# Two transformer blocks on one core: the last two output slabs by token halves, and the norm by pairs of chunks

## The chip, the cores and the metric

The kernel runs on one core of one Trainium2 chip. The metric is the device time of one execution in microseconds (us), lower is better. Each kernel is run several times and the median is given.

## What is computed

The reference runs two models one behind the other on 512 tokens with 1024 features, all in fp32. The first has two layers: a gated delta-net mixer and then a latent-attention (MLA) mixer, each followed by a gated feed-forward network (FFN). The second has one layer: retention and sliding-window attention merged by gates, and again an FFN. Around each of them stands the same pattern:

```python
h = rmsnorm(x, g) * (1.0 + scale) + shift
y = mixer(h)
x = x + gate * y
h = rmsnorm(x, g2) * (1.0 + scale2) + shift2
x = x + gate2 * swiglu(h, w_gate, w_up, w_down)
```

`rmsnorm` divides each token's vector by the root of the mean of its squares over the 1024 features. The second model has no shift and takes, in front of it, two norms in a row (the first model's final one and its own first one).

## The kernel before

**Layout.** x lies transposed in SBUF: 8 chunks (KC) of 128 features on the partitions, 512 tokens in the free dimension. A product of fp32 quality is made of three matmuls: every operand is split into a rounded high part and the low rest (`hi`, `lo` for weights, `hH`, `hL` for the normed activation, `aH`, `aL` for the hidden one), and lo*H, hi*L and hi*H are added up in PSUM. The weights come as slabs of 128x2048 (256 output features). SP loads a slab into `raw`, ScalarE rounds it to `hi` (`split_hi`, L362), VectorE subtracts to `lo` (`split_lo`, L366). There are two buffers of each (`raw0/1`, `hi0/1`, `lo0/1`) and two PSUM tiles D0 and D1 for slabs; D2 holds the sums of squares. `ones` times the squares on TensorE gives the sum over features on all partitions (`ones_half`, L583).

**Order.** There is no scheduler: each engine's program is written out by hand, and counting semaphores tie them together. `lo_ready` counts slabs whose low part is ready, `slab_done` slabs whose products are done, `out_half` the first halves of a junction's last slab, `x_added` and `bank_free` chunks added to x, `fsq_ready` squares, `fold_ready` folds, `fss_ready` sums, `xg_ready` normed chunks, `hh_ready` and `h_ready` high and low parts of the activation.

**A junction.** Six times a block ends with four output slabs (N_OUT) and the residual add, and a norm follows; five times the first slab of the next block follows that. In order of the program they are called here by what comes in front of or behind them: G_GOUT (n = 1, norm of the first FFN behind it), G_MIN (n = 2, the end of the first FFN and the norm of the MLA mixer), G_MOUT (n = 3), G_RET (n = 4, two norms in a row, two sums of squares at once), G_ROUT (n = 6), and the kernel's end (n = 7). The functions are `final_pe`, `final_act`, `final_dve` for the four slabs, `close_act`, `close_dve` for the norm (`last_act`, `last_dve` at the end), `product_halves` (L321) for the next block's first slab.

The first three slabs are multiplied with all 512 tokens per matmul (L301 to L303 in `product`), the last one by halves of 256 tokens (L611 to L613), so that the first half's norm can start while the second half is multiplied. VectorE adds a slab's two chunks to x (L557, by halves L721); ScalarE squares them (L619) into `af` or `sg`; VectorE folds the squares of two slabs into one (L644) and, before the last slab, the two chunks of the fold into one (L649). `ones_half` of a half adds one matmul of the fold and two of the last slab's squares. Then ScalarE takes Ln (L667) and Exp (L669) to get the reciprocal root for 256 tokens.

The norm handles 16 pieces (2 halves of tokens by 8 chunks, 128x256 each). For each of them VectorE multiplies x with gain and root into `nq` (L735), ScalarE adds the shift and rounds to `hH` (L706) and, where the next block's product by seven quarters wants the whole value (n = 1, 3, 6), writes it once more unrounded to `tR` (L708, L705), and VectorE adds the shift to `nq` again and subtracts `hH` to get `hL` (L742). `product_halves` waits for each piece's `h_ready`. `nq` has four places.

**Weights around a junction.** With slab 4 the first of the next block and slab 5 its second, `final_act` and `final_dve` split slabs 2, 3 and 4 while slabs 0, 1 and 2 are added; `close_act` rounds slab 5 at piece 6 of 16, `close_dve` takes its low part when all pieces are done. At the kernel's end slab 4 is a dummy of zeros, loaded and split like any other.

## Time and profile before

| | us |
|---|---|
| median of 3 runs | 2347.21 |
| lowest, highest | 2346.96, 2348.32 |
| the profiled execution | 2349.4 |
| its span, first to last instruction | 2347.6 |
| TensorE busy | 2266.1 (97%) |
| VectorE busy | 1401.0 (60%) |
| ScalarE busy | 1042.5 (44%) |
| GpSimd busy | 366.7 (16%) |

In the profile PE is TensorE, DVE VectorE, ACT ScalarE, POOL GpSimd. A matmul's duration in the records contains its way through the array, so matmuls overlap there: what one costs in a row of many is the distance from start to start. The same holds, to a smaller degree, for VectorE and ScalarE instructions that follow each other without a wait.

### The profile page before, as it was taken

To read this page: it belongs to the slowest core of one execution; us is meant where nothing else is said; L and a number is where in the kernel's file an instruction comes from. 1 tells how busy PE (TensorE), PEld (TensorE's weight loads), DVE (VectorE), ACT (ScalarE), POOL (GpSimd) and SP (SyncE) were. 2 spreads that over 40 slices of the span, in tenths; PEclk is the share of its full clock that TensorE was granted. 3 is DMA by queue.
4 is the path that set the end of the run, shared out by engine and by line. 5 is a ranking of instruction groups with operands and counts; after the bars stand their busy time and mean duration, and the time that the engine had idled before them with its cause. 6 is when DMAs were issued, how large, how long until landed. Compare 5 with 4: busy or idle time off the path is not lost.

```text
span 2347.6 us, 34925 instructions
## 1 busy us (share of the span) xinstructions
PE 2266.1 (97%) x14369; PEld 1920.9 (82%) x14369; DVE 1401.0 (60%) x1800; ACT 1042.5 (44%) x1568; POOL 366.7 (16%) x164
## 2 busy tenths in 40 slices
PE   6999999999999999999999999999999999999998
PEld 4777888878889986668998998888777788898897
DVE  4856755543347765547883676645367345984484
ACT  4546553443215444435552455334255325553352
POOL 0346447347790000000000000000000000000000
PEclk9999999999999999999999999999999999999999
DMA  7433232334452324311333233212211222233232
GB/s 294 143 116 135 100 135 91 118 115 181 181 210 90 109 73 163 130 67 54 109 108 117 83 124 110 85 62 72 90 55 56 89 90 72 91 108 126 90 108 90
DMA packets 40762, 260.56 MB, mean 111 GB/s; under 512 B 4432, under 2 KB 6832, under 8 KB 10416
## 3 DMA queue, kind: packets, MB, share of 16 engines
q1 hardware_dynamic: 40624, 258.59, 30.3%
q8 instruction: 103, 1.69, 0.3%
q14 instruction: 35, 0.29, 0.0%
HBM read 256.42 MB, written 2.15 MB: 110 GB/s over the span
## 4 chain that ended last, share of the span: by engine, by line
PE 79%; DVE 8%; ACT 5%; issue 2%; POOL 2%; DMA 0%; DVEq 0%; ACTq 0%
PE D L301 10%; PE D L303 10%; PE D L302 10%; PE D L1638 7%; PE D L1640 7%; PE D L1639 7%; PE D L1403 2%; PE D L2866 2%; PE D L1405 2%; PE D L1404 2%; DVE lo L366 1%; PE D L2868 1%; PE D L2867 1%; PE D L1422 1%; ACT hi L362 1%
## 5 line engine op out<-in xcount | busy, mean ns | idle before, releaser
L366 DVE TENSOR_TENSOR lo<-raw,hi 128x2048 fp32r<-128x2048 f32 (+3 forms) x131 | 288.9, 2205 | 200.4 <-ACT hi L362 200.2
L362 ACT ACTIVATE hi<-raw 128x2048 fp32r<-128x2048 f32 (+3 forms) x131 | 230.1, 1756 | 328.6 <-PE D L303 240.0
L301 PE MATMUL D<-hH,lo 128*128 128x512 f32 x560 | 227.3, 406 | 5.6 <-DVE lo L366 5.6
L303 PE MATMUL D<-hH,hi 128*128 128x512 f32 x560 | 220.9, 394 | 0.0
L302 PE MATMUL D<-hL,hi 128*128 128x512 f32 x560 | 220.9, 394 | 0.0
L1638 PE MATMUL D<-tH,lo 128*128 128x256 f32 x768 | 216.3, 282 | 0.5 <-issue 0.5
L1640 PE MATMUL D<-tH,hi 128*128 128x256 f32 x768 | 216.3, 282 | 0.0
L1639 PE MATMUL D<-tL,hi 128*128 128x256 f32 x768 | 216.2, 282 | 0.0
L375 POOL TENSOR_TENSOR adar<-adar 128x1024 f32<-128x1024 f32 (+2 forms) x120 | 213.2, 1777 | 9.4
L373 POOL TENSOR_TENSOR adar<-adar,small 128x2048 f32<-128x2048 f32 x40 | 154.0, 3850 | 326.5 <-DVE zi L1289 189.0
L1638 PE MATMUL D<-hH,lo 128*128 128x256 f32 x576 | 162.6, 282 | 2.3 <-ACT D L1721 2.3
L1640 PE MATMUL D<-hH,hi 128*128 128x256 f32 x576 | 162.1, 282 | 0.0
L1639 PE MATMUL D<-hL,hi 128*128 128x256 f32 x576 | 162.1, 281 | 0.0
L301 PE MATMUL D<-aH,lo 128*128 128x512 f32 x390 | 154.5, 396 | 0.0
L302 PE MATMUL D<-aL,hi 128*128 128x512 f32 x390 | 154.0, 395 | 0.0
L303 PE MATMUL D<-aH,hi 128*128 128x512 f32 x390 | 153.9, 395 | 0.0
L1638 PEld LDWEIGHTS D<-tH,lo 128*128 128x128 f32 x768 | 144.6, 188 | 1.1 <-issue 0.9
L1639 PEld LDWEIGHTS D<-tL,hi 128*128 128x128 f32 x768 | 144.6, 188 | 0.2
L1640 PEld LDWEIGHTS D<-tH,hi 128*128 128x128 f32 x768 | 144.6, 188 | 0.0
L301 PEld LDWEIGHTS D<-hH,lo 128*128 128x128 f32 x560 | 105.5, 188 | 32.8 <-DVE lo L366 7.2
L302 PEld LDWEIGHTS D<-hL,hi 128*128 128x128 f32 x560 | 105.5, 188 | 25.6 <-issue 2.4
L303 PEld LDWEIGHTS D<-hH,hi 128*128 128x128 f32 x560 | 105.4, 188 | 24.7
(537 smaller groups left out, 5481.7 us busy)
## 6 DMA issues: line engine op xcount, KB each, us to landing
raw<-in_slabs SPq DMA_DIRECT2D x185, 1024.0 KB, 4.8
adar<-in_ada SPq DMA_DIRECT2D x42, 1024.0 KB, 4.8
fw<-in_ada SPq DMA_DIRECT2D x6, 1024.0 KB, 24.0
x<-in_xin SPq DMA_DIRECT2D x2, 1024.0 KB, 8.9
dt<-bcast SPq DMA_DIRECT2D x8, 256.0 KB, 3.2
dtb<-bcast SPq DMA_DIRECT2D x8, 256.0 KB, 3.5
qd<-bcast SPq DMA_DIRECT2D x8, 256.0 KB, 3.7
out<-x SPq DMA_DIRECT2D x8, 256.0 KB, 2.2
```

The lines of the kernel that those rows point to most:

```text
L301: T_.matmul(o, lo[s.slot][:, w], H[:, k, :], start=(k == 0), stop=False)
L302: T_.matmul(o, hi[s.slot][:, w], L[:, k, :], start=False, stop=False)
L303: last = T_.matmul(o, hi[s.slot][:, w], H[:, k, :], start=False, stop=(k == kc - 1))
L362: S_.activation(hi[s.slot][:, 0:n], raw[s.slot][:, 0:n], ACT.Copy).then_inc(hi_ready, 1)
L366: V_.tensor_tensor(lo[s.slot][:, 0:n], raw[s.slot][:, 0:n], hi[s.slot][:, 0:n], ALU.subtract).then_inc(lo_ready, 1)
L373: chain.link(nc.gpsimd.tensor_tensor(r3, r3, cact.unsqueeze(2).to_broadcast([P, KC, 2 * P]), ALU.mult))
L375: last = nc.gpsimd.tensor_tensor(r3[:, 0:n], r3[:, 0:n], r3[:, n:2 * n], ALU.add)
L1403: T_.matmul(o, lo[s % 2][:, c], hH[:, k, :], start=(k == 0), stop=False)
L1404: T_.matmul(o, hi[s % 2][:, c], hL[:, k, :], start=False, stop=False)
L1638: T_.matmul(to, w(lo, k), H(k), start=(fresh and k == 0), stop=False, skip_group_check=True)
L1639: T_.matmul(to, w(hi, k), L(k), start=False, stop=False, skip_group_check=True)
L1640: last = T_.matmul(to, w(hi, k), H(k), start=False, stop=(k == 3), skip_group_check=True)
```

## The change

**Halves.** TensorE now takes the last two slabs by halves of the tokens, both first halves first: first half of slab 2, first half of slab 3, second half of slab 2, second half of slab 3. `out_half` counts two per junction.

**Squares.** The squares of slabs 0 and 1 are folded as before. The squares of slab 2 are folded in by halves (`half_fold_dve`); for the first half the two chunks of the fold are then folded once more into one of 256 columns, for the second half they are not. `ones_half` of the first half has 1 + 2 matmuls and stands after 36 of 48 matmuls of slab 2's second half; that of the second half has 2 + 2 and stands, as before, behind three chunks of the next block's first slab.

**Norm.** It goes by 8 pairs of chunks instead of 16 pieces. For n = 1, 2, 3 ScalarE writes a pair with the shift added to `tR` (two instructions) and rounds it to `hH` as one copy of 128x2x256; for n = 6, without a shift, VectorE writes `tR` itself and ScalarE only copies; for n = 4 VectorE multiplies with the root alone (one instruction of two chunks) and ScalarE applies the gain as it rounds. `hL` is one subtraction of two chunks (n = 4: two instructions). `h_ready` counts pairs.

**Weights.** Slab 4 is split in the norm instead of before it: ScalarE behind pair 0, VectorE behind pair 0's low part and the add of slab 2's second half. ScalarE rounds slab 5 behind all pairs. The dummy slab at the end is neither loaded nor split.

```diff
+            for h in range(2):
+                for j in range(N_OUT - 2, N_OUT):
+                    s = Slab(base + j)
+                    if h == 0:
+                        pe.wait_ge(lo_ready, s.plus(1))
+                        pe.wait_ge(bank_free[s.slot], s.prior())
+                    for m in range(2):
+                        o = D[s.slot][:, h, m * HT:(m + 1) * HT]
+                        for k in range(kc):
+                            if (h, j, m * kc + k) == (1, N_OUT - 2, 12):
+                                ones_half(pe, f, 0)
...
         def ones_half(pe, f, h):
-            pe.wait_ge(fold_ready, 3 * f + 3)
+            pe.wait_ge(fold_ready, 4 * f + h + 3)
             for q, (a, b) in enumerate(sums_of(f)):
                 o = D[2][:, h, q * HT:(q + 1) * HT]
-                T_.matmul(o, ones, a[:, 0, TH[h]], start=True, stop=False)
+                for m in range(h + 1):
+                    T_.matmul(o, ones, a[:, m, TH[h]], start=(m == 0), stop=False)
                 for m in range(2):
-                    pe.wait_ge(fsq_ready, 10 * f + 6 + 2 * h + m + 1)
+                    pe.wait_ge(fsq_ready, 12 * f + 4 * h + m + 7)
                     last = T_.matmul(o, ones, b[:, m, TH[h]], start=False, stop=(m == 1))
...
+            def pair(p):
+                act.wait_ge(xg_ready, XG[n] + p + 1)
+                if n == 4:
+                    for m in range(2):
+                        c = 2 * (p % 4) + m
+                        last = S_.activation(of_pair(hH, p)[:, m, :], norm_pair(p)[:, m, :], ACT.Identity, bias=shift(c),
+                                             scale=gain(c))
+                else:
+                    if n != 6:
+                        for m in range(2):
+                            last = S_.activation(whole_pair(p)[:, m, :], norm_pair(p)[:, m, :], ACT.Identity,
+                                                 bias=shift(2 * (p % 4) + m))
+                        last.then_inc(whole_ready, 1)
+                        act.wait_ge(whole_ready, WHOLE[n] + p + 1)
+                    last = S_.activation(of_pair(hH, p), whole_pair(p), ACT.Copy)
+                last.then_inc(hh_ready, 1)
             S_.preload_act_table_set("natural_log_exp_and_others")
-            half_squares_act(act, base, f, 0)
+            half_squares_act(act, base, f, 0, N_OUT - 1)
             half_rstd_act(act, f, n, 0)
...
+            pair(0)
+            split_hi(act, Slab(base + N_OUT))
+            half_squares_act(act, base, f, 1, N_OUT - 2)
+            pair(1)
+            pair(2)
+            half_squares_act(act, base, f, 1, N_OUT - 1)
+            pair(3)
+            half_rstd_act(act, f, n, 1)
+            for p in range(4, KC):
+                pair(p)
+            split_hi(act, Slab(base + N_OUT + 1))
...
             half_rstd_dve(dve, n, 0)
...
+            normed(0)
+            normed(1)
+            rest(0)
+            half_adds_dve(dve, base, gate, f, 1, N_OUT - 2)
+            split_lo(dve, Slab(base + N_OUT))
+            half_fold_dve(dve, f, 1)
+            normed(2)
+            rest(1)
+            normed(3)
+            rest(2)
+            half_adds_dve(dve, base, gate, f, 1, N_OUT - 1)
+            rest(3)
+            half_rstd_dve(dve, n, 1)
+            normed(4)
+            normed(5)
+            rest(4)
...
```

In `last_dve` four of the first half's eight scalings now stand ahead of the add of slab 2's second half, four behind its fold, and all eight ahead of the add of the last slab's second half.

How the instructions stand on ScalarE in G_MOUT's norm. In the kernel before slab 5 (`hi1`) is rounded in the middle, two pieces ahead of the second half's Ln and Exp:

```order
L362 ACTIVATE hi1<-raw1 128x2048
L706 ACTIVATE hH<-nq,mod 128x256
L708 ACTIVATE tR<-nq,mod 128x256
L706 ACTIVATE hH<-nq,mod 128x256
L708 ACTIVATE tR<-nq,mod 128x256
L667 ACTIVATE nrs<-D2,vec 128x256
L669 ACTIVATE nrs<-nrs 128x256
L706 ACTIVATE hH<-nq,mod 128x256
L708 ACTIVATE tR<-nq,mod 128x256
```

And in the changed kernel, the last three pairs (and the slab behind them):

```order
L729 ACTIVATE tR<-nq,mod 128x256 x2
L733 ACTIVATE hH<-tR 128x2x256
L729 ACTIVATE tR<-nq,mod 128x256 x2
L733 ACTIVATE hH<-tR 128x2x256
L729 ACTIVATE tR<-nq,mod 128x256 x2
L733 ACTIVATE hH<-tR 128x2x256
L361 ACTIVATE hi1<-raw1 128x2048
```

The rounding of slab 5 has moved from ahead of the first half's last two pieces to behind the last pair.

On VectorE, at the start of the same norm. Before, slab 4's low part (`lo0`) and both folds stand ahead of the add of the last slab's first half:

```order
L557 SCALAR_TENSOR_TENSOR x<-D0,mod,x 128x512 x2
L366 TENSOR_TENSOR lo0<-raw0,hi0 128x2048
L644 TENSOR_TENSOR af<-af,sg 128x1024
L649 TENSOR_TENSOR af<-af 128x512
L721 SCALAR_TENSOR_TENSOR x<-D1,mod,x 128x256 x2
L735 SCALAR_TENSOR_TENSOR nq<-x,gsc,nrs 128x256 x2
L742 SCALAR_TENSOR_TENSOR hL<-nq,mod,hH 128x256
```

In the changed kernel:

```order
L655 SCALAR_TENSOR_TENSOR x<-D1,mod,x 128x256 x2
L765 SCALAR_TENSOR_TENSOR nq<-x,gsc,nrs 128x256 x4
L775 TENSOR_TENSOR hL<-tR,hH 128x2x256
L655 SCALAR_TENSOR_TENSOR x<-D0,mod,x 128x256 x2
L365 TENSOR_TENSOR lo0<-raw0,hi0 128x2048
L663 TENSOR_TENSOR af<-af,sg 128x2x256
L765 SCALAR_TENSOR_TENSOR nq<-x,gsc,nrs 128x256 x2
L775 TENSOR_TENSOR hL<-tR,hH 128x2x256
L765 SCALAR_TENSOR_TENSOR nq<-x,gsc,nrs 128x256 x2
L775 TENSOR_TENSOR hL<-tR,hH 128x2x256
L655 SCALAR_TENSOR_TENSOR x<-D1,mod,x 128x256 x2
L775 TENSOR_TENSOR hL<-tR,hH 128x2x256
```

Slab 4's low part has moved behind pair 0's low part, and the add of the last slab's second half (D1, the row before the last) stands behind pair 2's.

## Rows read from the trace of the kernel before

**Rows 1.** The page's first part: busy time of each engine.

```profile
PE 2266.1 (97%) x14369; PEld 1920.9 (82%) x14369; DVE 1401.0 (60%) x1800; ACT 1042.5 (44%) x1568; POOL 366.7 (16%) x164
```

**Rows 2.** Waits of PE: waited for; us in total, times, longest.

```profile
PE D L333 <- DVE hL L742: 13.2, 13, 2.2
```

**Rows 3.** Timeline of PE, junction G_MOUT: start, us, instruction [idle before].

```profile
1058.52 0.40 PE L301 MATMUL D<-hH,lo 128*128 128x512 f32 x1
...
1069.72 0.28 PE L611 MATMUL D<-hH,lo 128*128 128x256 f32 x1
...
1077.92 0.59 PE L588 MATMUL D<-af,cst 128*128 128x256 f32 x2
...
1079.33 0.28 PE L612 MATMUL D<-hL,hi 128*128 128x256 f32 x1
...
1089.52 0.38 PE L333 MATMUL D<-hH,lo 128*128 128x256 f32 x1 [1.36 <-DVE hL L742]
...
1100.79 0.50 PE L301 MATMUL D<-hH,lo 128*128 128x512 f32 x1 [1.23 <-DVE lo L366]
```

**Rows 4.** Timeline of ACT, G_MOUT, and one row of G_MIN (849.52).

```profile
1060.60 1.14 ACT L619 ACTIVATE sg<-x 128x512 f32<-128x512 f32 x2
...
1079.41 0.47 ACT L667 ACTIVATE nrs<-D,vec 128x256 f32<-128x256 f32 x1 [2.09 <-PE D L591]
1079.92 0.42 ACT L669 ACTIVATE nrs<-nrs 128x256 f32<-128x256 f32 x1
...
1086.66 1.90 ACT L362 ACTIVATE hi<-raw 128x2048 fp32r<-128x2048 f32 x1
1088.46 0.49 ACT L706 ACTIVATE hH<-nq,mod 128x256 fp32r<-128x256 f32 x1
...
849.52 0.91 ACT L706 ACTIVATE hH<-nq,mod 128x256 fp32r<-128x256 f32 x2 [0.55 <-DVE nq L735]
```

**Rows 5.** Timeline of DVE, G_MOUT.

```profile
1075.39 0.69 DVE L649 TENSOR_TENSOR af<-af 128x512 f32<-128x512 f32 x1
1076.00 0.87 DVE L721 SCALAR_TENSOR_TENSOR x<-D,mod,x 128x256 f32<-128x256 f32 x2
...
1080.37 0.88 DVE L735 SCALAR_TENSOR_TENSOR nq<-x,gsc,nrs 128x256 f32<-128x256 f32 x2 [3.50 <-ACT nrs L669]
...
1090.99 0.88 DVE L735 SCALAR_TENSOR_TENSOR nq<-x,gsc,nrs 128x256 f32<-128x256 f32 x2 [0.73 <-ACT nrs L669]
...
1098.45 2.28 DVE L366 TENSOR_TENSOR lo<-raw,hi 128x2048 fp32r<-128x2048 f32 x1
```

**Rows 6.** Timeline of PE, the other junctions: slab 2 and slab 5 start.

```profile
449.80 0.40 PE L301 MATMUL D<-hH,lo 128*128 128x512 f32 x1
...
492.36 0.50 PE L301 MATMUL D<-hH,lo 128*128 128x512 f32 x1 [0.88 <-DVE lo L366]
...
827.19 0.40 PE L301 MATMUL D<-aH,lo 128*128 128x512 f32 x1
...
867.31 0.50 PE L301 MATMUL D<-hH,lo 128*128 128x512 f32 x1 [1.18 <-DVE lo L366]
...
1416.41 0.40 PE L301 MATMUL D<-aH,lo 128*128 128x512 f32 x1
...
1455.92 0.58 PE L333 MATMUL D<-hH,lo 128*128 128x256 f32 x1 [2.15 <-DVE hL L742]
...
1463.63 0.38 PE L353 MATMUL D<-hi,hL 128*128 128x256 f32 x1 [0.27 <-DVE lo L366]
...
1955.81 0.40 PE L301 MATMUL D<-hH,lo 128*128 128x512 f32 x1
...
1998.00 0.50 PE L301 MATMUL D<-hH,lo 128*128 128x512 f32 x1 [1.23 <-DVE lo L366]
```

**Rows 7.** Timeline of PE and DVE at the kernel's end.

```profile
2337.58 0.59 PE L588 MATMUL D<-af,cst 128*128 128x256 f32 x2
...
2338.71 0.75 DVE L721 SCALAR_TENSOR_TENSOR x<-D,x 128x256 f32<-128x256 f32 x2
```

**Rows 8.** Stretch in G_RET: busy times, PEclk (granted clock), DMA share, GB/s.

```profile
1455.90:1459.10 3.20, 3.18 (x15) 3.18 (x16) 3.20 (x9) 1.95 (x4) 0.00 (x0) 0.50 0.98 362
```

More of the change, by code:

```diff
@@ L594, in final_pe @@
         def final_pe(pe, base, kc, H, L, ready, f, begun=False):
-            for j in range(N_OUT - 1):
+            for j in range(N_OUT - 2):
                 s = Slab(base + j)
@@ new lines, in final_act, with half_adds_dve @@
+            half_squares_act(act, base, f, 0, N_OUT - 2)
+        def half_adds_dve(dve, base, gate, f, h, j):
+            s = Slab(base + j)
+            if h:
+                dve.wait_ge(slab_done, s.plus(1))
+            else:
+                dve.wait_ge(out_half, 2 * f + j - 1)
+            for m in range(2):
+                c = 2 * j + m
+                xc = x[:, c, TH[h]]
+                V_.scalar_tensor_tensor(out=xc, in0=D[s.slot][:, h, m * HT:(m + 1) * HT], scalar=gate(c) if gate else 1.0,
+                                        in1=xc, op0=ALU.mult, op1=ALU.add).then_inc(
+                    bank_free[s.slot] if h and m else x_added, 1)
@@ new lines, in half_fold_dve @@
+        def half_fold_dve(dve, f, h):
+            dve.wait_ge(fsq_ready, 12 * f + 4 * h + 6)
+            dve.wait_ge(fold_ready, 4 * f + 1)
+            for a, b in sums_of(f):
+                last = V_.tensor_tensor(a[:, :, TH[h]], a[:, :, TH[h]], b[:, :, TH[h]], ALU.add)
+            last.then_inc(fold_ready, 1)
+            if h == 0:
+                dve.wait_ge(fold_ready, 4 * f + 2)
+                for a, b in sums_of(f):
+                    last = V_.tensor_tensor(a[:, 0, TH[0]], a[:, 0, TH[0]], a[:, 1, TH[0]], ALU.add)
+                last.then_inc(fold_ready, 1)
@@ L634, in final_dve @@
         def final_dve(dve, base, gate, f):
-            for j in range(N_OUT - 1):
+            for j in range(N_OUT - 2):
                 s = Slab(base + j)
@@ L3270, in _ @@
             final_act(act, G_MOUT, 2)
-            close_act(act, G_MOUT, 2, 3, col(mod, MD(1, 3)))
+            close_act(act, G_MOUT, 2, 3, col(gsc, 3 * KC), col(mod, MD(1, 3)))
             quick_act(act, G_FFN1, 1, 3)
-            close_act(act, G_RET - N_OUT, 3, 4, zero)
+            close_act(act, G_RET - N_OUT, 3, 4, col(gsc, KC), zero)
             act.wait_ge(tab_in, 64)
```

205 lines of the change are left out of this document (91 added, 114 removed).

## The prediction, on record before the changed kernel was run

> **What bounds the kernel now.** Page first: TensorE is busy 97% of the span [rows 1], so the time is TensorE's work plus the places where it waits. Then the table of TensorE's waits [rows 2]: its first entry is the first product after a norm (L333) waiting for the norm's low parts (hL), 13.2 us in 13 waits. These lie in the five junctions (end of one block, norm, first slab of the next) which the change rewrites; a sixth stands at the end. Last the timelines of one junction, that of G_MOUT. I count T from the first matmul of its second to last slab, 1058.52 [rows 3]. TensorE starts the last slab at T = 11.20, the ones block at 19.40, and the next block's second slab at T = 42.27. In between stand waits of 1.36 us (high parts queued behind a 1.90 us rounding of weights on ScalarE [rows 4]) and, at the end, 1.23 us for the weights' low part, which VectorE starts at 1098.45, when the last hL is done [rows 5]. So a junction's length is set by the chain statistics, norm, weights; the kernel gains or loses what T = 42.27 gains or loses.
>
> **The prices.** A slab of 48 matmuls of 512 columns takes 11.20. Of 256 columns, 69 lie between 1069.72 and 1077.92: 0.119 each, 5.70 for the 48 of half a slab [rows 3]. Hence TensorE has done with the last slab at 11.20 + 11.40 + 1.29 = 23.9. A ones block of three matmuls: 1077.92 to 1079.33 less one step of 0.12 = 1.29, so 0.43 each [rows 3]. VectorE, start to start: a chunk of 256 from SBUF 0.40 (two take 0.88, the first ends at 0.48), from PSUM 0.40 as well, a TENSOR_TENSOR of 512 0.61 (1075.39 to 1076.00) [rows 5]. ScalarE: a chunk of 256 0.40 (two take 0.91); 512 elements 0.52 (two take 1.14, one 0.615); a wait for its own result 0.04 (L667 ends at 1079.88, L669 starts at 1079.92); rounding a slab 1.82, done after 1.91 [rows 4]. Across engines I take 0.03 to 0.08 (L669 ends at 1080.34, VectorE starts at 1080.37 [rows 4, 5]), and 0.1 for the first matmul after a wait, whose record is 0.38 long instead of 0.28 [rows 3].
>
> Checked on the order of before, a walk with these prices gives 42.24, 40.15, 42.13 and 46.8 where the rows give 42.27, 40.12, 42.19 and 47.22 [rows 3, 6]; the last is the norm of two sums, and I add 0.4 there.
>
> **The change, part by part.**
> *Halves.* Two slabs in four half blocks: 22.8 instead of 22.6 before; +0.2 per junction.
> *Ones.* The second half's block has four matmuls instead of three: +0.43.
> *Norm by pairs.* The rounding as one copy of two chunks (128x2x256) isn't in the trace. Bounds: 0.40, a single chunk, and 0.62, the whole of a 512 activation; nearest is the 512 activation start to start, 0.52, and I take 0.54. A pair costs ScalarE 0.80 + 0.14 (end of the second, own wait) + 0.54 = 1.5 instead of 4 x 0.40 = 1.6; VectorE 0.80 + 0.61 = 1.41 instead of 1.6; TensorE uses a pair in 12 x 0.119 = 1.43. With the copy at 0.40 or 0.62 the four pairs on the path move the end by -0.6 or +0.3.
> The Trainium skill ("VectorE: DVE Perf Modes", section on the TRN2 errata) gives ScalarE from SBUF 224 cycles plus the elements at 1.2 GHz, thus 0.61 for 512: by it the pair is 0.07 dearer and a junction 0.3 longer, an estimate; the trace's back-to-back 512 activations are faster than that.
> *Weights.* Rounding of the next block's first slab moves from the last slab's start into the norm (ScalarE after pair 0, VectorE after pair 0's rest), that of its second slab from the middle of the norm to its very end. SP: the slab loads behind them wait for those low parts, but have over 10 us until used; hidden. The dummy load at the end goes; nobody waits for it.
>
> **The walk, G_MOUT.** Half blocks of TensorE end at 5.70, 11.40; the weights of the last slab must be ready at 5.70 instead of 11.2: VectorE has them at 4.4. VectorE adds the last slab's first half at 11.6, ScalarE squares by 12.9; but TensorE asks for the sums only at 15.67 (after 36 matmuls), ends them at 16.96; Ln, Exp until 18.05; norm starts at 18.1 instead of 21.85 (1080.37). So the start is 3.8 earlier. Then: pair 0 high at 20.6, rest 20.6 to 21.3; ScalarE rounds weights 20.5 to 22.4; VectorE adds the second half of slab 3 of 4 (21.2 to 22.1), low weights 22.4 to 24.7. TensorE is free at 24.1 (23.9 + 0.2) and **waits 0.7 for the weights**. VectorE: fold 24.6, pair 2's norm 25.2, pair 1's rest 26.0 to 26.7: **wait 0.5**. The last slab's second half is added behind pair 2's rest, 28.4 to 29.2, squared by 29.7; TensorE, which has asked for it at 27.6 and done two ones matmuls, **waits 0.9**. Ones end 30.3. ScalarE is in pair 3 until 31.1, Ln and Exp until 32.0, so half two's norm starts at 32.0, where before it started at 32.5 (1090.99, 32.47): of 3.8 us only half a microsecond is left. Pair 4 is ready at 35.25, TensorE free at 33.9: **wait 1.4**. Pairs at 1.5 bring pair 7's high part at 39.3; only then ScalarE rounds weights (39.2 to 41.1), VectorE 41.1 to 43.4: the second slab starts at **43.5, 1.2 later than now**, after a wait of 2.0.
>
> **The other junctions**, same walk. G_GOUT has the same instructions and stands at 42.56 now: +0.9. G_MIN: now no chunk is written to tR, ScalarE has slack and T is 40.12 [rows 6]; the change writes tR there too and ends at 43.5: **+3.4**. G_RET (two sums, norm in one multiply of 0.61): norm at 21.2, weights low 24.7 to 27.0, second statistics 35.4, norm 38.3, pair 7 high 44.0, weights 43.9 to 48.2, plus the 0.4: 48.6 against 47.22: +1.4. G_ROUT (no shift: VectorE writes tR, ScalarE only copies, 0.54 per pair): product starts without a wait at 24.1, waits 0.3 and 0.65, second statistics 29.2, norm 30.3, last weights 35.6 to 39.8: 39.9 against 42.19: **-2.3**. End of the kernel: the last add waits for VectorE's eight scalings until 2338.71, though TensorE has come to the ones at 2337.58 [rows 7]: an add that follows TensorE within 0.2 would start at 2337.8. Now VectorE has its scalings behind it by then, so the add is 0.9 earlier, less the 0.2: -0.7.
> Sum: 0.9 + 3.4 + 1.2 + 1.4 - 2.3 - 0.7 = **+3.9 us**. The profiled execution took 2349.4 (span 2347.6), the median of the runs is 2347.21, 2.2 below; the difference is laid on the median: **2351.1 us**.
>
> **Rivals.**
> *A clock fall (slower).* The new waits before the second slabs are 2.0 us. At G_RET a wait of 2.15 was followed by a stretch at the granted clock 0.50, the 1.2 GHz level [rows 6, 8]; where the waits are 1.36 and shorter, no such stretch shows. At G_RET the stretch cost little, since VectorE set the pace; behind a second slab TensorE sets it. 3.2 us at half speed lose 1.6. One to three such falls (G_GOUT, G_MIN, G_MOUT): 2352.7 to 2355.9. For: the wait's size. Against: 2.0 is less than 2.15, and at G_RET the wait came shortly after others.
> The Trainium skill ("TensorE: Matmul & The Clock Gate", Terms) puts the penalty at the throttled time times (1 - K/N), half of it: 1.6 for this row; G_RET's end moved by under 0.4, so for that row it is an upper bound, and behind a second slab the two agree.
> *ScalarE doesn't bind (faster).* If a pair took it about 1.1 or less, the end would follow statistics and VectorE as in G_ROUT, and the 3.8 us earlier start would pay: G_GOUT, G_MIN and G_MOUT at 39.9 as well, -2.7, -0.2, -2.4; with +1.4 - 2.3 - 0.7 that is -6.9: 2340.3. It decides at the copy: the next instruction would have to start 0.15 after it, and the cheapest row is 0.40.
> *The halves don't come early.* If the last slab's weights were late (needed at 5.70, ready at 4.4, in G_GOUT beside GpSimd a microsecond later), TensorE would wait there, 0.5 at most: inside the forecast's range.
>
> **Chances.** A measurement tells about 0.2% (4.7 us) from no change. Forecast without a clock fall 0.62: mostly 2349 to 2353, with the copy's bounds times three junctions (-1.8, +1.2) and about 1 us each way for walks; 0.14 of it lies over 2351.9. Clock falls 0.28, nearly all of it slower or close. ScalarE not binding 0.08. Late weights 0.02. So slower 0.41, same 0.50, faster 0.09. The range takes in three falls at its upper end, and the cheap copy (-1.8) with 2.5 for the walks at its lower; it leaves out the faster rival: 2346.8 to 2356.0.
>
> **What the profile would show.** Right: the first Ln about 17.2 after the second to last slab's start; waits of about 0.7 for lo, then 0.5, 0.9 (in the ones) and 1.4 in the first product, and about 2.0 before the second slab, whose weights ScalarE rounds after the last copy; G_ROUT shorter than 40.5; G_MIN longer than 42.5. Wrong: a copy start to start under 0.45, or G_MIN below 41.5; then ScalarE was not the engine that ends the chain.

## The result, and the profile after

Timed in alternation on one chip, the changed kernel took 2352.14 us in the median of 16 runs, the kernel before 2348.11 us (median of 16); the ratio is 1.0016 with a 95% interval of 1.0009 to 1.0023. Fifteen of the 16 runs lie between 2349.44 and 2355.09 (their median is 2351.91); one took 7211.88 us at a mean granted clock of 0.284 and is not counted in the ratio. Timed again beside other kernels the ratio was 1.0023 (1.0013 to 1.0033). So the change is slower by 0.16 to 0.23%, some 4 to 5 us, against a forecast of +3.9 us and 2351.1. Neither interval holds 1, but the difference is about as large as the 0.2% that the prediction took for the least a measurement can tell. The profiled execution has a span of 2350.8 us (before: 2347.6).

The first line of its page's busy times answers to [rows 1]: 302 matmuls and 3.6 us more on TensorE.

```profile
PE 2269.7 (97%) x14671; PEld 1937.1 (82%) x14671; DVE 1396.6 (59%) x1778; ACT 1037.0 (44%) x1549; POOL 365.4 (16%) x164
```

TensorE's waits (what was waited for; us in total, times, longest). The 13.2 us of [rows 2] have become 4.3 and, at G_RET (hL of L780), 2.6 us. In their place stand longer waits for weights and sums. L300 is the first matmul of a whole slab, which waits for that slab's low weights (5.6 us in 6 waits before); L332 is `product_halves`, which waits for hL or for the first slab's weights (the latter is new); L591 is the ones block (2.3 us before). All rows of this view add up to some 74 us before and 73 after.

```profile
PE D L300 <- DVE lo L365: 6.9, 6, 1.7
...
PE D L332 <- DVE hL L775: 4.3, 6, 1.2
...
PE D L332 <- DVE lo L365: 3.5, 4, 1.8
PE D L591 <- ACT sg L621: 3.0, 5, 0.8
...
PE D L332 <- DVE hL L780: 2.6, 2, 2.1
```

TensorE's timeline in G_MOUT (start, us, instruction, idle time before it and what ended it). It answers to [rows 3]; T counts from 1061.33.

```profile
1061.33 0.29 PE L613 MATMUL D<-hH,lo 128*128 128x256 f32 x1
...
1077.18 0.59 PE L588 MATMUL D<-af,cst 128*128 128x256 f32 x2
...
1086.31 0.39 PE L332 MATMUL D<-hH,lo 128*128 128x256 f32 x1 [0.56 <-DVE lo L365]
...
1088.30 0.39 PE L332 MATMUL D<-hH,lo 128*128 128x256 f32 x1 [0.31 <-DVE hL L775]
...
1090.94 1.13 PE L591 MATMUL D<-sg,cst 128*128 128x256 f32 x4 [0.78 <-ACT sg L621]
...
1096.79 0.39 PE L332 MATMUL D<-hH,lo 128*128 128x256 f32 x1 [1.12 <-DVE hL L775]
...
1104.96 0.50 PE L300 MATMUL D<-hH,lo 128*128 128x512 f32 x1 [1.71 <-DVE lo L365]
```

All five forecast waits are there, each a little shorter: 0.56, 0.31, 0.78, 1.12 and 1.71 us for 0.7, 0.5, 0.9, 1.4 and 2.0. The second slab starts at T = 1104.96 - 1061.33 = 43.63.

ScalarE's timeline there, which answers to [rows 4]: statistics (L690, L692), the copies in tR (L729), the rounding as one copy of two chunks (L733), weights (L361).

```profile
1078.67 0.47 ACT L690 ACTIVATE nrs<-D,vec 128x256 f32<-128x256 f32 x1 [4.29 <-PE D L591]
...
1081.49 0.63 ACT L733 ACTIVATE hH<-tR 128x512 fp32r<-128x512 f32 x1
1082.03 1.90 ACT L361 ACTIVATE hi<-raw 128x2048 fp32r<-128x2048 f32 x1
...
1087.68 0.91 ACT L729 ACTIVATE tR<-nq,mod 128x256 f32<-128x256 f32 x2 [1.68 <-DVE nq L765]
...
1090.47 0.75 ACT L621 ACTIVATE sg<-x 128x256 f32<-128x256 f32 x2 [1.21 <-DVE x L655]
...
1094.44 0.91 ACT L729 ACTIVATE tR<-nq,mod 128x256 f32<-128x256 f32 x2 [0.95 <-DVE nq L765]
...
1095.92 0.89 ACT L729 ACTIVATE tR<-nq,mod 128x256 f32<-128x256 f32 x2
...
1100.69 1.90 ACT L361 ACTIVATE hi<-raw 128x2048 fp32r<-128x2048 f32 x1
```

The copy takes 0.54 from start to start (1081.49 to 1082.03), a pair 1.48 (1094.44 to 1095.92). The second slab's weights are rounded at 1100.69, behind pair 7, and TensorE waits for what VectorE makes of them. The rows also hold what the prediction passed over: ScalarE stands idle for 1.68 and 1.21 us between the halves, waiting for VectorE.

VectorE there, which answers to [rows 5]: the norm of the two halves (L765), the last slab's second half added (L655), the second slab's low weights (L365).

```profile
1079.63 1.68 DVE L765 SCALAR_TENSOR_TENSOR nq<-x,gsc,nrs 128x256 f32<-128x256 f32 x4 [5.70 <-ACT nrs L692]
...
1089.89 0.87 DVE L655 SCALAR_TENSOR_TENSOR x<-D,mod,x 128x256 f32<-128x256 f32 x2
...
1093.52 1.68 DVE L765 SCALAR_TENSOR_TENSOR nq<-x,gsc,nrs 128x256 f32<-128x256 f32 x4
...
1102.62 2.29 DVE L365 TENSOR_TENSOR lo<-raw,hi 128x2048 fp32r<-128x2048 f32 x1 [1.11 <-ACT hi L361]
```

Two other junctions on TensorE, which answer to [rows 6]: G_MIN and G_ROUT from the second to last slab's start to the second slab's.

```profile
828.18 0.28 PE L613 MATMUL D<-aH,lo 128*128 128x256 f32 x1
...
871.79 0.50 PE L300 MATMUL D<-hH,lo 128*128 128x512 f32 x1 [1.71 <-DVE lo L365]
...
1961.95 0.28 PE L613 MATMUL D<-hH,lo 128*128 128x256 f32 x1
...
2001.84 0.50 PE L300 MATMUL D<-hH,lo 128*128 128x512 f32 x1 [1.05 <-DVE lo L365]
```

From such rows come the T of all junctions. "End" is the time from the second to last slab's first matmul to the end of the span. "MLA" is the stretch from G_MIN's second slab to G_MOUT's second to last one, which the change doesn't touch. Where a kernel was profiled twice, both are shown.

| kernel | G_GOUT | G_MIN | G_MOUT | G_RET | G_ROUT | end | MLA |
|---|---|---|---|---|---|---|---|
| before | 42.56 | 40.12 | 42.27 | 47.22 | 42.19 | 33.88 | 191.21 |
| forecast | 43.5 | 43.5 | 43.5 | 48.6 | 39.9 | -0.7 | |
| after | 43.63 | 43.61 | 43.63 | 49.16 | 39.89 | 33.30 | 189.54 |
| after_again | 43.45 | 43.62 | 43.44 | 50.31 | 39.89 | 33.30 | 189.55 |
| e1_w5_mid | 42.80 | 42.69 | 42.68 | 48.16 | 38.87 | 33.29 | 191.19 |
| e2_min_plain | 43.54 | 41.55 | 43.44 | 49.15 | 40.07 | 33.30 | 191.11 |
| e2_again | 43.66 | 41.54 | 43.46 | 50.41 | 39.89 | 33.29 | 191.07 |
| e3_pairs_only | 43.40 | 43.06 | 42.96 | 48.69 | 38.16 | 33.86 | 191.11 |
| e4_no_pairs | 44.80 | 44.68 | 44.88 | 49.15 | 40.07 | 33.29 | 191.09 |
| e5_add_early | 42.20 | 42.19 | 42.37 | 47.63 | 39.10 | 33.30 | 189.56 |
| e6_best | 41.34 | 38.48 | 40.63 | 47.70 | 37.49 | 33.30 | 191.11 |
| e6_again | 41.39 | 38.48 | 40.79 | 47.69 | 37.49 | 33.31 | 191.13 |
| e7_old_halves_ordered | 41.61 | 38.74 | 40.81 | 48.26 | 37.28 | 33.88 | 189.74 |

After less before the junctions give 1.07 + 3.49 + 1.36 + 1.94 - 2.30 - 0.58 = +5.0 us, and the MLA stretch takes 1.67 back: together 3.3, where the spans differ by 3.2. What that 1.67 is stands in a view of the windows of the kernel after (us; busy time and instructions of PE, PEld, DVE, ACT, POOL; then the granted clock, the DMA share, GB/s):

```profile
1019.90:1023.40 3.50, 3.50 (x16) 1.81 (x15) 1.61 (x6) 0.82 (x3) 0.00 (x0) 1.00 0.53 225
1042.70:1046.20 3.50, 3.50 (x13) 3.00 (x12) 0.00 (x0) 0.60 (x1) 0.00 (x0) 0.51 0.00 0
```

and the same view of the kernel before:

```profile
1015.40:1018.90 3.50, 3.50 (x10) 1.93 (x10) 0.86 (x4) 0.85 (x3) 0.00 (x0) 0.51 0.50 213
1039.30:1042.80 3.50, 3.50 (x14) 3.21 (x15) 0.00 (x0) 0.60 (x1) 0.00 (x0) 0.51 0.00 0
```

Before the change the stretch has two pieces at half clock (the windows of 3.5 us show 0.51; half clock is the 1.2 GHz level), after it one. The first of before starts 148.1 us behind G_MIN's second slab (867.31, [rows 6]); 148.1 us behind 871.79 is 1019.90, and there the changed kernel runs at full clock. TensorE has the same waits in front of these places in both kernels. Timelines of TensorE, the kernel after:

```profile
1019.41 0.33 PE L2352 MATMUL D<-cst,pr 128*128 128x128 f32 x1 [1.52 <-DVE pr L2529]
...
1042.08 0.65 PE L2352 MATMUL D<-cst,pr 128*128 128x128 f32 x4 [1.94 <-DVE pr L2529]
```

and the kernel before:

```profile
1014.93 0.33 PE L2295 MATMUL D<-cst,pr 128*128 128x128 f32 x1 [1.55 <-DVE pr L2472]
...
1039.20 1.03 PE L2295 MATMUL D<-cst,pr 128*128 128x128 f32 x4 [1.94 <-DVE pr L2472]
```

So the wait of 1.55 us was followed by half clock, the one of 1.52 was not.

### The profile page after: what moved, and what is told of

Its sections match the earlier page's. It is cut to its first block, busy times and chain, and to the rows that moved or that the text cites. A ratio compares the mean times of both kernels' runs of the same rounds, so it can differ in the third digit from the quotient of the medians.

```text
span 2350.8 us, 35446 instructions
## 1 busy us (share of the span) xinstructions
PE 2269.7 (97%) x14671; PEld 1937.1 (82%) x14671; DVE 1396.6 (59%) x1778; ACT 1037.0 (44%) x1549; POOL 365.4 (16%) x164
## 3 DMA queue, kind: packets, MB, share of 16 engines
HBM read 255.38 MB, written 2.15 MB: 110 GB/s over the span
## 4 chain that ended last, share of the span: by engine, by line
PE 79%; DVE 7%; ACT 5%; issue 3%; POOL 2%; DMA 0%; DVEq 0%; ACTq 0%
PE D L300 9%; PE D L301 9%; PE D L302 9%; PE D L1696 7%; PE D L1698 7%; PE D L1697 7%; PE D L1461 2%; PE D L2923 2%; PE D L1463 2%; PE D L1462 2%; ACT hi L361 1%; PE D L614 1%; PE D L615 1%; PE D L613 1%; PE D L2925 1%
## 5 line engine op out<-in xcount | busy, mean ns | idle before, releaser
L365 DVE TENSOR_TENSOR lo<-raw,hi 128x2048 fp32r<-128x2048 f32 (+3 forms) x130 | 286.7, 2205 | 203.8 <-ACT hi L361 203.5
L361 ACT ACTIVATE hi<-raw 128x2048 fp32r<-128x2048 f32 (+3 forms) x130 | 228.1, 1754 | 280.0 <-PE D L302 191.7
L300 PE MATMUL D<-hH,lo 128*128 128x512 f32 x512 | 208.3, 407 | 6.9 <-DVE lo L365 6.9
L302 PE MATMUL D<-hH,hi 128*128 128x512 f32 x512 | 201.9, 394 | 0.0
L301 PE MATMUL D<-hL,hi 128*128 128x512 f32 x512 | 201.9, 394 | 0.0
L300 PE MATMUL D<-aH,lo 128*128 128x512 f32 x342 | 135.5, 396 | 0.0
L301 PE MATMUL D<-aL,hi 128*128 128x512 f32 x342 | 135.0, 395 | 0.0
L302 PE MATMUL D<-aH,hi 128*128 128x512 f32 x342 | 135.0, 395 | 0.0
L300 PEld LDWEIGHTS D<-hH,lo 128*128 128x128 f32 x512 | 96.5, 188 | 31.9 <-DVE lo L365 8.5
L301 PEld LDWEIGHTS D<-hL,hi 128*128 128x128 f32 x512 | 96.5, 188 | 23.4 <-issue 2.4
L302 PEld LDWEIGHTS D<-hH,hi 128*128 128x128 f32 x512 | 96.4, 188 | 22.5
```

Of the source, the lines that this page charges most:

```text
L300: T_.matmul(o, lo[s.slot][:, w], H[:, k, :], start=(k == 0), stop=False)
L301: T_.matmul(o, hi[s.slot][:, w], L[:, k, :], start=False, stop=False)
L302: last = T_.matmul(o, hi[s.slot][:, w], H[:, k, :], start=False, stop=(k == kc - 1))
L361: S_.activation(hi[s.slot][:, 0:n], raw[s.slot][:, 0:n], ACT.Copy).then_inc(hi_ready, 1)
L365: V_.tensor_tensor(lo[s.slot][:, 0:n], raw[s.slot][:, 0:n], hi[s.slot][:, 0:n], ALU.subtract).then_inc(lo_ready, 1)
```

## The experiments

The theory at that point: the junctions' length is set by what ScalarE and VectorE do between the statistics and the second slab's weights, in the order written down for them, and by the copies in tR. The rival came with the page of the profile: TensorE is busy 3.6 us longer, its waits add up to about the same, and the kernel is 4 us slower, which would be the whole story without any order. A second rival is the clock. Differences are to the kernel before, timed beside each; the changed kernel stands at +4.0 and +4.9.

**e1_w5_mid: the second slab's weights between the halves.**

```
             pair(2)
+            split_hi(act, Slab(base + N_OUT + 1))
             half_squares_act(act, base, f, 1, N_OUT - 1)
...
             for p in range(4, KC):
                 pair(p)
-            split_hi(act, Slab(base + N_OUT + 1))
```

> ScalarE rounds the weights of the next block's second slab (split_hi of N_OUT + 1) between pair 2 and the last slab's second half of squares, instead of after pair 7. Nothing else moves. T is the time after the first matmul of the second to last slab. Theory (the junction's length is set by ScalarE, whose last act is that rounding): the wait of 1.7 us before the second slab goes, the slab starts at T = 42.8 instead of 43.6 at G_GOUT, G_MIN and G_MOUT, 47.6 to 48.1 instead of 49.2 at G_RET, 38.7 instead of 39.9 at G_ROUT; the second statistics come later by what the rounding pushes back, so only 0.8 of the 1.7 is gained. Together -4.4 us against the changed kernel: 2347.7. Rival A (the 4 us lost are TensorE's own added work, 3.6 us of busy time in ones blocks and halves): the order on ScalarE changes nothing, 2352. Rival B (the clock falls are the loss): 2350 to 2352, with the T of G_GOUT, G_MIN and G_MOUT unchanged.

Measured: 2348.26 us, ratio 1.0003 (0.9994 to 1.0012), which is +0.3 us to before and about 4 less than the changed kernel. T is 42.80, 42.69, 42.68, 48.16, 38.87: each within 0.2 of the theory's. ScalarE now rounds the weights in the pause between the halves, and TensorE's wait before the second slab falls from 1.71 to 0.51 (timelines of ScalarE and TensorE in G_MOUT):

```profile
1086.16 1.89 ACT L361 ACTIVATE hi<-raw 128x2048 fp32r<-128x2048 f32 x1
```

```profile
1101.21 0.50 PE L300 MATMUL D<-hH,lo 128*128 128x512 f32 x1 [0.51 <-DVE lo L365]
```

TensorE has the same 14671 matmuls as in the changed kernel, and the loss is all but gone: the added work can be carried without it. So the rival falls as the whole story. TensorE's busy time is 2265.2 us here, less than before the change, so it doesn't follow the number of matmuls alone.

**e2_min_plain: no copy in tR at G_MIN**, where nobody reads it.

```
+                if n == 2:
+                    for m in range(2):
+                        last = S_.activation(of_pair(hH, p)[:, m, :], norm_pair(p)[:, m, :], ACT.Identity,
+                                             bias=shift(2 * (p % 4) + m))
...
+                if n == 2:
+                    dve.wait_ge(xg_ready, XG[n] + p + 1)
+                    for m in range(2):
+                        c = 2 * (p % 4) + m
+                        last = V_.scalar_tensor_tensor(out=hL[:, c, TH[p // 4]], in0=norm_pair(p)[:, m, :], scalar=shift(c),
+                                                       in1=hH[:, c, TH[p // 4]], op0=ALU.add, op1=ALU.subtract)
```

> At G_MIN alone no copy in tR is written: ScalarE rounds the two chunks of a pair straight from the norm (two of 256), VectorE takes the rest by two SCALAR_TENSOR_TENSOR of 256, as before the change. Theory: G_MIN lost 3.5 us because ScalarE has 1.5 us per pair where 0.8 would do; without the copies VectorE sets the pace (1.6 per pair) and the second slab starts at T = 41.5 instead of 43.6; the other junctions stay at 43.6, 43.6, 49.2, 39.9. Total -2.0 against the changed kernel: 2350.1. Rival A (TensorE's added work): 2352, T at G_MIN unchanged.

Measured: T at G_MIN 41.55, as the theory has it, but 2352.21 us, ratio 1.0017 (1.0008 to 1.0026): nothing gained, a miss of the total by 2. The table shows where it went: the MLA stretch is 191.12 us instead of 189.54. So it was run once more, beside the changed kernel.

> The kernel without the copy in tR at G_MIN once more. Its junction was 2.1 us shorter, its time was not (2352.2). Theory (the difference lies in short clock falls elsewhere, which come or not from run to run and kernel to kernel, 1.6 each; its profile showed one at 1568.7 and two between G_MIN and G_MOUT where the changed kernel's showed none and one): the T of the junctions repeat within 0.2 us, the number or places of the falls don't, and the median may lie anywhere between 2349.5 and 2352.5. Rival (the time gained at G_MIN is given back by a wait further on in the block that follows): the stretch from G_MIN to G_MOUT is longer than the changed kernel's by 1.6 again, with a wait of TensorE in it.

> The changed kernel once more, beside the others on one chip. Theory: 2351 to 2353, the T of the junctions as before within 0.2 us, the clock falls of 3.5 us at other places or in another number, so that the stretches between junctions differ by multiples of 1.6. Rival: the stretches repeat, falls included, since each kernel has its own fixed set.

Measured: 2350.64 us, ratio 1.0013 (1.0004 to 1.0022), and 2352.19 us for the changed kernel, 1.0023 (1.0013 to 1.0033). The expectation that the falls wouldn't repeat was wrong: the stretch is 191.07 again, and 189.55 again for the changed kernel. The rival was wrong in its cause, since TensorE's long waits in the stretch are the same in both kernels (1.95, 1.53 and 1.94 us, within 0.02). It is the clock, in the same two places of the program in both runs; the view of windows of e2_again:

```profile
907.40:910.90 3.50, 3.50 (x11) 2.68 (x10) 0.69 (x1) 0.00 (x0) 0.00 (x0) 0.52 0.74 260
1016.60:1020.10 3.50, 3.38 (x11) 2.31 (x11) 1.41 (x6) 1.22 (x5) 0.00 (x0) 0.51 0.64 260
```

With one such piece in the changed kernel and two here, of the 2.1 us gained in the junction 1.5 are given back. Not everything repeated: G_RET takes 50.41 and 50.31 us for 49.15 and 49.16 the first time, with a piece of 6.9 us at half clock in it instead of shorter ones, and the first e2 has a piece at 1568.7 that the second has not.

**e3_pairs_only: pairs alone.** The functions final_pe, final_act, final_dve, ones_half, half_squares_act, half_adds_dve, last_act and last_dve are those of before, close_dve is put in order for them (the last slab's second half is added behind pair 2's norm, earlier than in the changed kernel), and in close_act:

```
+            half_squares_act(act, base, f, 0)
             half_rstd_act(act, f, n, 0)
             pair(0)
-            split_hi(act, Slab(base + N_OUT))
-            half_squares_act(act, base, f, 1, N_OUT - 2)
             pair(1)
+            half_squares_act(act, base, f, 1)
             pair(2)
-            half_squares_act(act, base, f, 1, N_OUT - 1)
+            split_hi(act, Slab(base + N_OUT + 1))
             pair(3)
...
-            split_hi(act, Slab(base + N_OUT + 1))
```

> The order of the last two slabs, the folds, the ones blocks and the end of the kernel are those of before; the norm by pairs is kept, with the weights of the second slab rounded after pair 2. Theory: the halves in the new order bring the first statistics 3.8 us earlier but bind nothing, so pairs alone, with the weights in the middle, give T = 43.0 at the three junctions with a copy in tR, 46.2 to 47.1 at G_RET, 38.3 at G_ROUT: -5.2 against the changed kernel at the junctions, +0.6 at the kernel's end, 2347.5; by half a microsecond each it is even shorter than the changed kernel at every junction. Rival A (TensorE's added work is what was lost): the 3.6 us of it go, and with them nothing else: 2348.5, with waits of TensorE as in the changed kernel. The two are told apart by T and waits rather than by the total.

Measured: 2350.80 us, ratio 1.0008 (0.9999 to 1.0017), 1.2 to 2.1 below the changed kernel where both theories had 3.6 and more. The three junctions with copies in tR are at 43.40, 43.06 and 42.96, G_ROUT at 38.16, within 0.4 of the expected; G_RET is at 48.69 instead of 46.2 to 47.1, a miss. There the profile has a piece at half clock right behind a wait of 2.58 us, at 1449.70:

```profile
1449.70:1453.20 3.50, 3.44 (x16) 3.47 (x17) 2.91 (x6) 2.43 (x7) 0.00 (x0) 0.51 0.00 0
```

The later run with this order of the slabs (e7, below) has the same wait (2.59), half clock behind it as well, and G_RET at 48.26: no run shows this G_RET without the piece, so what it costs there isn't shown. Against the rival: with the old 14369 matmuls TensorE is busy 2269.7 us, as long as in the changed kernel with its 14671 (e3 has five pieces at half clock between the first junction and G_ROUT, the changed kernel three, e1 two), and the waits are other ones (1.16, 0.55, 0.89, 1.65 and 0.49 us in G_MOUT). The page's line for e3:

```profile
PE 2269.7 (97%) x14369; PEld 1924.0 (82%) x14369; DVE 1394.6 (59%) x1760; ACT 1036.7 (44%) x1536; POOL 365.0 (16%) x164
```

The edit moves three things against the changed kernel: the halves, the second slab's weights and VectorE's add. The nearest kernel with the new halves is e1, which has the weights in nearly the same place: there the second slab starts 0.3 to 0.6 us earlier than here at four junctions and 0.7 later at G_ROUT. So the new halves are worth a little, 0.2 us in the mean of the five, and taking their work away gains nothing but at G_ROUT.

**e4_no_pairs: the rounding undone, the halves kept.** Two chunks in tR and two high parts, four activations of 256, and the rest by two instructions:

```
+                elif n != 6:
+                    for to in (whole_pair(p), of_pair(hH, p)):
+                        for m in range(2):
+                            last = S_.activation(to[:, m, :], norm_pair(p)[:, m, :], ACT.Identity,
+                                                 bias=shift(2 * (p % 4) + m))
```

> The new order of halves is kept, but the rounding is undone: at G_GOUT, G_MIN and G_MOUT ScalarE writes two chunks of the copy and two high parts, four activations of 256 from the norm (1.6 us per pair instead of 1.5), and VectorE takes the rest by two instructions of 256. G_RET and G_ROUT stay. Theory (ScalarE's load sets the end): T = 44.7 at those three instead of 43.6, +3.8 in all against the changed kernel (a part of it VectorE's, which also has 1.6 instead of 1.4 per pair): 2355.9. Rival A (TensorE's added work): 2352, nothing moves. Rival C (the pairs themselves are what costs, by the wait for ScalarE's own result): it becomes faster than the changed kernel, 2350 or less.

Measured: 2357.11 us, ratio 1.0036 (1.0022 to 1.0050), 9.1 above before and 4 to 5 above the changed kernel. T is 44.80, 44.68 and 44.88 for the expected 44.7; G_RET and G_ROUT stay. A pair takes ScalarE 1.62 where the changed kernel has 1.48 (1101.90 to 1103.52):

```profile
1101.90 0.91 ACT L728 ACTIVATE tR<-nq,mod 128x256 f32<-128x256 f32 x2
1102.72 0.90 ACT L728 ACTIVATE hH<-nq,mod 128x256 fp32r<-128x256 f32 x2
1103.52 1.90 ACT L361 ACTIVATE hi<-raw 128x2048 fp32r<-128x2048 f32 x1
```

Against four activations per pair the rounding as one copy is a gain, of some 1.2 us per junction at these three, VectorE's part with it; it isn't what costs. The total is 1.2 above the expected, and the MLA stretch is at 191.08.

**e5_add_early: VectorE's add of the last half earlier.** It stood behind pair 3's norm and pair 2's rest.

```
+            half_adds_dve(dve, base, gate, f, 1, N_OUT - 1)
             normed(3)
             rest(2)
-            half_adds_dve(dve, base, gate, f, 1, N_OUT - 1)
             rest(3)
```

> VectorE adds the last slab's second half (half_adds of 1, N_OUT - 1) before pair 3's norm instead of behind pair 2's rest; nothing else moves. Theory: that add waits on VectorE for instructions which it doesn't need (0.8 us of TensorE's wait in the ones block); 1.4 us earlier it brings the second statistics earlier, and as ScalarE's work on the second half can start only then, T of the next block's second slab is 42.2 instead of 43.6 at G_GOUT, G_MIN and G_MOUT, 47.5 instead of 49.2 at G_RET, 39.1 instead of 39.9 at G_ROUT, with the wait of 1.7 before that slab as it is: -6 against the changed kernel, 2346. Rival (TensorE's added work is the loss, or ScalarE is busy without a pause from the first statistics on, so that an earlier end of the sums buys nothing): 2351 to 2352.

Measured: 2344.95 us, ratio 0.9992 (0.9983 to 1.0001): 7 us below the changed kernel, a little more than the 6 expected. T is 42.20, 42.19, 42.37, 47.63, 39.10. The add starts at 1085.26 and TensorE's wait in the ones block is gone; the one before the second slab stays at 1.72. Timelines of VectorE and TensorE:

```profile
1085.26 0.86 DVE L655 SCALAR_TENSOR_TENSOR x<-D,mod,x 128x256 f32<-128x256 f32 x2
```

```profile
1100.79 0.50 PE L300 MATMUL D<-hH,lo 128*128 128x512 f32 x1 [1.72 <-DVE lo L365]
```

```profile
1089.36 1.67 DVE L765 SCALAR_TENSOR_TENSOR nq<-x,gsc,nrs 128x256 f32<-128x256 f32 x4
```

That last row, of VectorE again, is the second half's norm: T = 1089.36 - 1058.42 = 30.94, 1.25 earlier than in the changed kernel (32.19), and the second slab starts 1.26 earlier. One moved line is worth more than the whole change cost: the moment of the second statistics sets the end, whichever engine holds them up.

**e6_best: an order for each junction**, with no copy in tR at G_MIN. `s2` and `a2` are the second half's squares and add of the second to last slab, `s3` and `a3` the last slab's, `w4` and `w5` the weights of the first and second slab, `p`, `n`, `r` the pairs' high part, norm and rest, `R` the statistics, `f` the fold.

```
ScalarE
 1, 3: "R0 w4 p0 s2 p1 p2 s3 p3 R1 w5 p4 p5 p6 p7"
 2:    "R0 w4 p0 s2 p1 p2 s3 p3 R1 p4 p5 w5 p6 p7"
 4:    "R0 p0 w4 p1 s2 w5 p2 s3 p3 R1 p4 p5 p6 p7"
 6:    "R0 p0 w4 p1 s2 w5 s3 p2 p3 R1 p4 p5 p6 p7"
VectorE
 1, 3: "R0 n0 a2 n1 w4 r0 n2 r1 f1 a3 n3 r2 r3 R1 n4 n5 r4 n6 r5 n7 r6 r7 w5"
 2:    "R0 n0 a2 n1 w4 r0 r1 n2 f1 a3 n3 r2 r3 R1 n4 n5 r4 r5 n6 n7 r6 r7 w5"
 4:    "R0 n0 n1 a2 r0 n2 w4 r1 f1 a3 n3 r2 r3 R1 n4 n5 r4 r5 n6 n7 r6 r7 w5"
 6:    "R0 n0 n1 a2 r0 w4 f1 r1 a3 n2 n3 r2 r3 R1 n4 n5 r4 r5 n6 n7 r6 r7 w5"
```

> The changed kernel with an order of its own for each junction, written as a list of steps for ScalarE and one for VectorE: the next block's first weights are rounded before pair 0 or pair 1 (ScalarE has nothing to do there), the second slab's between the halves or earlier, the adds of the second halves before the norm's steps that stand in their way, and at G_MIN no copy in tR. TensorE's order is untouched. Theory (orders and load of ScalarE and VectorE set the junctions): T = 40.7, 38.5, 40.7, 46.0, 37.4 instead of 43.6, 43.6, 43.6, 49.2, 39.9, -16.7 against the changed kernel, 2335 to 2336, which beats both kernels by half a per cent. Each clock fall more or less is worth 1.6. Rival (TensorE's added work is the loss, orders don't matter): 2351 to 2352. Between them: where two engines hand over too finely for the walk, 2340.

Measured: 2337.28 us, ratio 0.9963 (0.9949 to 0.9976), 10 us below before and 15 below the changed kernel; 16.7 were expected. Three junctions are where they should be (38.48, 40.63, 37.49), G_GOUT and G_RET are 0.7 and 1.7 too long. At G_GOUT TensorE waits 1.86 us before the product's second half, and then runs at half clock (timeline of TensorE, and windows):

```profile
482.39 0.40 PE L332 MATMUL D<-hH,lo 128*128 128x256 f32 x1 [1.86 <-DVE hL L793]
```

```profile
482.60:486.10 3.50, 3.50 (x18) 3.50 (x18) 2.83 (x6) 3.22 (x7) 0.00 (x0) 0.51 0.02 5
```

At G_MOUT the same order has the same wait (1.89) and no such piece, and T is 0.7 shorter. Two more lie in G_RET.

**e7_old_halves_ordered: the same with the old halves.** Since most of the gain so far came from orders, the last question was what the halves are worth: pairs and an order for each junction, but one whole slab and one by halves, folds and ones blocks as before.

```
ScalarE
 1, 3:    "R0 p0 p1 s3 w5 p2 R1 p3 p4 p5 p6 p7"
 2, 4, 6: "R0 p0 p1 w5 s3 p2 p3 R1 p4 p5 p6 p7"
VectorE
 1, 3:    "R0 n0 n1 a3 r0 n2 r1 n3 w5 r2 R1 n4 r3 n5 r4 n6 r5 n7 r6 r7"
 2:       "R0 n0 n1 r0 a3 r1 n2 n3 r2 r3 R1 n4 n5 r4 r5 n6 n7 r6 r7 w5"
 4, 6:    "R0 n0 n1 r0 r1 a3 n2 n3 r2 r3 R1 n4 n5 r4 r5 n6 n7 r6 r7 w5"
```

> The pair norm with an order of its own for each junction, as in e6_best, and no copy in tR at G_MIN, but the last two slabs, folds and ones blocks are those of before (one slab whole, the last one by halves). It asks what the new order of halves is worth once ScalarE's and VectorE's orders are chosen for it. Theory (what sets a junction is the two engines' work between the statistics, so an earlier first half changes little): T = 40.8, 38.7, 40.8, 45.3 to 47, 37.1, against 40.7, 38.5, 40.7, 46.0 (47.7 with its clock falls), 37.4 in e6_best; with 0.6 us more at the kernel's end 2337 to 2339. Rival (the halves carry the gain, 3.8 us earlier first statistics at each junction): T longer than in e6_best by 1 to 3 us at each, 2343 to 2350.

> e6_best once more, on the chip of e7_old_halves_ordered: 2335 to 2339, T as before within 0.2 us where no clock fall lies in the junction. Its G_RET had 47.7 with two clock falls, its G_GOUT 41.3 with one behind a wait of 1.86; if they come again at the same places, they belong to this order, if not, to the run.

Measured: 2337.29 us, ratio 0.9956 (0.9942 to 0.9969), beside 2338.79 us for e6 again, ratio 0.9960 (0.9946 to 0.9973). The two can't be told apart, and their T differ by 0.6 at most. The expectation missed G_GOUT (41.61 for 40.8) and G_RET (48.26 for 45.3 to 47). In G_MOUT of this kernel TensorE waits longer for the first half (1.66 and 1.07 us) and then not at all: the second slab starts without an entry of idle time.

```profile
1077.34 0.36 PE L332 MATMUL D<-hH,lo 128*128 128x256 f32 x1 [1.66 <-DVE hL L783]
...
1082.82 0.39 PE L332 MATMUL D<-hH,lo 128*128 128x256 f32 x1 [1.07 <-DVE hL L783]
...
1092.44 0.40 PE L300 MATMUL D<-hH,lo 128*128 128x512 f32 x1
```

The rival, by which the halves carry the gain with 1 to 3 us at each junction, falls. They aren't worth nothing either: over the five junctions and the end e6 is 1.6 us shorter than e7 (e6_again 1.4). But its MLA stretch is 1.4 us longer, with two pieces at half clock for one, and so is the stretch from G_RET's second slab to G_ROUT, by 1.2 to 1.3 us, with one piece for none.

And e6_again has its clock pieces at the same places as e6_best, 481.5, 1437.3 and 1450.9 for 482.6, 1438.3 and 1452.0, with its G_GOUT starting 1.3 us earlier: these belong to the order, not to the run.

## Why the prediction was right, and where it was off

**The sum, +3.9 us against +4.0 and +4.9: right, and for its reasons in most terms.** G_GOUT +1.07 (forecast +0.9), G_MIN +3.49 (+3.4), G_MOUT +1.36 (+1.2), G_ROUT -2.30 (-2.3), end -0.58 (-0.7). The first Ln came at T = 1078.67 - 1061.33 = 17.34 (forecast 17.2), the first norm at 18.30 (18.1), the second at 32.19 (32.0), the last weights' rounding at 39.36 (39.2). Of 3.55 us by which the first norm is earlier than in [rows 5], the second norm keeps 0.28. That the halves' lead is lost between the two statistics is why they bring no gain. The loss itself comes behind them: from the second norm to the second slab it was 42.27 - 32.47 = 9.80 us and is 43.63 - 32.19 = 11.44, with the weights rounded last.

**The copy at 0.54: right.** It is 0.54 and at times 0.58 from start to start. By the Trainium skill ("VectorE: DVE Perf Modes", the section on the TRN2 errata) an activation of 512 would take 0.61, an estimate; the record's own length is 0.63, but the next one starts after 0.54, and a chain is paid by starts.

**ScalarE as the engine that ends the chain: right for the copies, too narrow for the rest.** e4 shows the load (0.1 us more per pair, 1.2 per junction), e2 the copies at G_MIN (2.1), e1 the weights rounded last (0.8 to 1.0 per junction). But e5 leaves ScalarE's order alone and gains more than e1 (6.4 us over the junctions for 4.7) by moving one add on VectorE: ScalarE had 1.68 and 1.21 us of idle time between the halves. The prediction named that add ("added behind pair 2's rest") and its wait of 0.9, and didn't ask what it cost behind.

**The rival "ScalarE doesn't bind": rightly given little.** All its junctions would be at 39.9; only G_ROUT is, where ScalarE just copies.

**The rival of a clock fall: the mechanism is real, its place was wrong.** None came behind the waits of 1.37 to 1.71 us before the second slabs. In the changed kernel's junctions they lie in G_RET alone, one more than before. The second sits behind a wait of 2.14 us as in [rows 8]:

```profile
1448.90:1452.30 3.40, 2.98 (x14) 2.69 (x13) 3.37 (x8) 1.09 (x2) 0.00 (x0) 0.51 0.00 0
1462.60:1466.00 3.40, 3.40 (x19) 3.40 (x18) 3.00 (x8) 2.64 (x5) 0.00 (x0) 0.50 1.00 380
```

These two cost nothing: e4, with the same work there, has no such piece in G_RET, longer waits of TensorE instead (0.90 and 0.97 us for 0.41 and 0.17) and the same 49.15. In after_again the first is 6.9 us long, and G_RET takes 50.31, 1.15 more. The prediction also went by the size of the wait (half clock behind 2.15 us, none behind 1.36 and shorter), and the trace that it had shows more: before the change there is half clock behind waits of 1.55 and 1.94 us in the MLA stretch, and none behind one of 2.31 us at 1562.83.

**G_RET, +1.94 instead of +1.4: a term was mis-sized.** The prediction took 0.40 for every chunk of 256 on ScalarE. At G_RET the high part is written with a gain and a shift from tables. ScalarE's timeline has four of these in 2.07 us, where e2_min_plain has four with a shift alone in 1.71. Timelines of ScalarE, e2_min_plain:

```profile
860.14 1.71 ACT L723 ACTIVATE hH<-nq,mod 128x256 fp32r<-128x256 f32 x4 [0.95 <-DVE nq L769]
```

and the changed kernel at G_RET:

```profile
1460.17 2.07 ACT L724 ACTIVATE hH<-nq,vec,gsc 128x256 fp32r<-128x256 f32 x4 [0.76 <-DVE nq L760]
...
1465.45 1.90 ACT L361 ACTIVATE hi<-raw 128x2048 fp32r<-128x2048 f32 x1
```

That is 0.49 per chunk, and 1.09 for a pair as against 0.91. Two such pairs stand on the path behind the second norm, the first and the last (between them ScalarE waits for VectorE): the rounding of the weights comes 6.0 us behind that norm instead of 5.6. The norm itself is late by 0.5 (T = 38.78 for 38.3), so that the last weights are rounded at T = 44.79 instead of 43.9; the 0.4 that the prediction added at the end covered a part of it. Which term made the norm late wasn't tried.

**What the prediction left out: the block behind.** It laid the junctions' difference on the whole time. The MLA stretch gave back 1.67 us by one clock fall fewer, and that is why the sum of the junctions, +5.0, was not the difference of the spans, +3.2. That the forecast met the total so closely is in part luck: it was 1.1 us short over the junctions, half of it at G_RET, and the stretch gave back what the forecast hadn't counted.

**What stays open.** Why the falls of the clock come at one place and not at another one with an equal wait (1.86 at G_GOUT, 1.89 at G_MOUT in e6) was not settled (nor why behind 1.55 us before the change and not behind 1.52 after it); no kernel was made that shifts only the start of a junction. How much of G_RET's 48.69 in e3 and 48.26 in e7 is the clock isn't known either.

## What to carry to other kernels

Work that comes earlier on one engine is worth what the next meeting point keeps of it: here 3.6 us at the first statistics became 0.3 at the second, and a kernel with the old halves and well chosen orders was as fast as one with the new, whose 1.5 us of shorter junctions went into more half clock elsewhere. Before a structural change, look for the idle gaps of the helper engines between two such points and for what is queued ahead of the instruction that ends them; one moved line on VectorE gained 7 us. A difference in TensorE's busy time isn't a count of work: it also holds what the clock costs. A copy for a later reader belongs only in the places that have such a reader. And when a junction gets shorter by a few microseconds, compare the stretches that you didn't touch as well.
